# One comparison in place of two: building the one-hot rows of a scatter from a shared key table

## The reference, cut to what matters

```python
idx = jnp.take_along_axis(cand_i, best_p, axis=-1)      # first key * 128 + second key
gate = jax.nn.softmax(best_s, axis=-1)
...
act = jnp.einsum('td,thkd->thk', xb, u_tab[ib])
wgt = jax.nn.gelu(act) * gb
return jnp.einsum('thk,thkd->td', wgt, v_tab[ib])
```

## Time and profile before

| | before |
|---|---|
| median of three runs | 3481.14 us (3479.04 to 3497.25) |
| the profiled execution, its own time | 3481.03 us |
| its span in the trace | 3479.0 us |
| scatter stage of the first layer, from its first comparison to the end of its last early multiply | 1673.30 to 1767.97 us |
| scatter stage of the second layer, likewise | 2730.77 to 2825.36 us |

### The profile page before, as it was taken

How to read it: one execution, slowest core, us unless ns; L and a number is a source line. 1 busy time by engine, 2 the same in 40 slices (tenths; PEclk the granted TensorE clock), 3 DMA queues, 4 the chain that set the end, 5 groups by cost and what they waited for, 6 DMA issues and landing times. The chain is left out here.

```text
span 3479.0 us, 65019 instructions
## 1 busy us (share of the span) xinstructions
PE 3333.5 (96%) x20516; PEld 2887.0 (83%) x20516; DVE 2443.6 (70%) x4853; ACT 1766.0 (51%) x3349; POOL 522.9 (15%) x428
## 2 busy tenths in 40 slices
PE   7999999999989998999899999999999889999999
PEld 5767776778769998889778999998789778999998
DVE  6657776767566775569877777776659877777776
ACT  4443343333356655646754545444656754454544
POOL 0000000000000001558720000000648730000000
PEclk9989999999999998999999999999999999999999
DMA  5125434435215554335045555555335135555554
GB/s 206 40 76 177 164 130 133 139 121 164 73 61 175 165 175 153 110 124 173 18 139 187 187 187 187 187 187 178 122 111 169 48 109 188 187 186 187 187 187 157
DMA packets 139223, 508.82 MB, mean 146 GB/s; under 512 B 15968, under 2 KB 16352, under 8 KB 138208
## 3 DMA queue, kind: packets, MB, share of 16 engines
q1 hardware_dynamic: 138384, 504.56, 45.0%
q10 hardware_dynamic: 720, 2.71, 0.2%
HBM read 506.16 MB, written 1.05 MB: 146 GB/s over the span
## 5 line engine op out<-in xcount | busy, mean ns | idle before, releaser
L286 ACT ACTIVATE split<-ring 128x512 fp32r<-128x512 f32 (+1 forms) x1700 | 1061.4, 628 | 1393.1 <-PE ps L217 1328.5
L293 DVE TENSOR_TENSOR split<-ring,split 128x512 fp32r<-128x512 f32 (+1 forms) x1404 | 956.9, 686 | 638.5 <-ACT split L286 617.1
L217 PE MATMUL ps<-h2T,split 128*128 128x256 f32 x7776 | 982.2, 284 | 7.6 <-DVE gates L2006 4.7
L217 PEld LDWEIGHTS ps<-h2T,split 128*128 128x128 f32 x7776 | 964.9, 192 | 29.5 <-DVE gates L2006 5.1
L217 PE MATMUL ps<-split,chunk 128*128 128x512 f32 x3072 | 735.3, 391 | 2.8 <-DVE chunk L2535 2.8
L293 POOL TENSOR_TENSOR split<-ring,split 128x512 fp32r<-128x512 f32 x296 | 389.4, 1332 | 2239.9 <-ACT split L286 2233.4
L217 PEld LDWEIGHTS ps<-split,chunk 128*128 128x128 f32 x3072 | 563.8, 188 | 113.9 <-DVE chunk L2535 4.0
L217 PE MATMUL ps<-hT,split 128*128 128x512 f32 (+1 forms) x3504 | 635.9, 341 | 9.7 <-DVE split L293 5.8
L217 PEld LDWEIGHTS ps<-hT,split 128*128 128x128 f32 x3504 | 537.3, 188 | 106.2 <-DVE hT L529 13.1
L2391 PE MATMUL ps<-ring 128*128 128x128 f32 x1024 | 146.8, 288 | 42.6 <-POOL ring L2379 27.1
L217 PE MATMUL ps<-act_chunk,split 128*128 128x512 f32 (+1 forms) x1056 | 186.1, 337 | 0.0
(11 more groups left out here) (348 smaller groups left out, 3133.4 us busy)
## 6 DMA issues: line engine op xcount, KB each, us to landing
ring<-peer_uv SPq DMA_DIRECT2D x456, 512.0 KB, 3.5
ring<-w_up SPq DMA_DIRECT2D x88, 512.0 KB, 3.8
ring<-w_choose SPq DMA_DIRECT2D x88, 512.0 KB, 3.6
ring<-w_mixing SPq DMA_DIRECT2D x68, 512.0 KB, 3.5
ring<-w_merge SPq DMA_DIRECT2D x64, 512.0 KB, 4.2
ring<-w_down SPq DMA_DIRECT2D x44, 512.0 KB, 3.6
mix_row_ring<-w_mod SPq DMA_DIRECT2D x40, 512.0 KB, 3.6
ffn_row_ring<-w_mod SPq DMA_DIRECT2D x40, 512.0 KB, 4.0
```

Source lines behind the costliest of these rows:

```text
L217: ins = nc.tensor.matmul(out, lhsT(a), rhs(b), start=first and n == 0, stop=last and n == len(PASSES) - 1)
L286: self.nc.scalar.activation(self.split[:, s % SPLIT, 0, cols], self.ring[:, s, cols], ACT.Copy).then_inc(self.high_ready, 1)
L293: (ops or self.nc.vector).tensor_tensor(self.split[:, s % SPLIT, 1, cols], self.ring[:, s, cols], self.split[:, s % SPLIT, 0, cols].bitcas ...
```

## The change

First and second keys go to one table, `slot_key`, in which each lot's four first keys and four second keys lie side by side; the one-hot rows lie in one tile, `hot`, lot by lot, first four rows of first keys, then four of second keys. With this DVE compares `iota` with seven keys (896 wide) in a single instruction, which raises `one_hot` once. The eighth row stays on ACT and is now the second key of the lot's last token. POOL waits for the one comparison, as PE does.

```diff
-RAW, SPLIT = 4, 2
+RAW, SPLIT, LOT = 4, 2, 4
...
-            for n, x in enumerate((k.slot_i, k.slot_j, k.slot_gate)):
-                nc.vector.tensor_copy(x[:, :], k.ps[:, RAW + n, 0:SEQ]).then_inc(slots_ready, 1)
+            for n, x in enumerate((k.slot_key[:, :, 0, :], k.slot_key[:, :, 1, :], k.slot_gate.rearrange("p (l t) -> p l t", t=LOT))):
+                nc.vector.tensor_copy(x, k.ps[:, RAW + n, 0:SEQ].rearrange("p (l t) -> p l t", t=LOT)).then_inc(slots_ready, 1)
...
-    on_act = 1
+    many = 2 * lot - 1
...
+    slot_keys = k.slot_key.rearrange("p l s t -> p (l s t)")
...
-                for hot, slot, first in ((k.hot_i, k.slot_i, 0), (k.hot_j, k.slot_j, on_act)):
-                    many = lot - first
-                    keys = slot[:, bass.ds(token(i, n) + first, many)].unsqueeze(2).broadcast_to([P, many, NK])
-                    nc.vector.tensor_tensor(hot[:, n * lot + first:(n + 1) * lot, :], iota[:, 0:many, :], keys,
-                                            ALU.is_equal).then_inc(one_hot, 1)
+                keys = slot_keys[:, bass.ds(token(i, n) * 2, many)].unsqueeze(2).broadcast_to([P, many, NK])
+                nc.vector.tensor_tensor(k.hot[:, n, 0:many, :], iota, keys, ALU.is_equal).then_inc(one_hot, 1)
...
-                    pool.wait_ge(one_hot, (i * lots + n) * 2 + 1)
-                    hot = k.hot_i[:, n * lot:(n + 1) * lot, :]
+                    pool.wait_ge(one_hot, i * lots + n + 1)
+                    hot = k.hot[:, n, 0:lot, :]
...
-                    pe.wait_ge(one_hot, (i * lots + n) * 2 + 2)
+                    pe.wait_ge(one_hot, i * lots + n + 1)
...
-                hot = k.hot_j[:, n * lot, :]
+                hot = k.hot[:, n, 2 * lot - 1, :]
...
-                                     bias=k.slot_j[:, bass.ds(token(i, n), 1)]).then_inc(distance, 1)
+                                     bias=slot_keys[:, bass.ds(token(i, n) * 2 + 2 * lot - 1, 1)]).then_inc(distance, 1)
...
-    k.slot_i, k.slot_j, k.slot_gate = (sb(scope, f"slot_{n}", SEQ) for n in ("i", "j", "gate"))
+    k.slot_key, k.slot_gate = sb(scope, "slot_key", SEQ // LOT, 2, LOT), sb(scope, "slot_gate", SEQ)
...
-    k.hot_i, k.hot_j = hot(16, NK), hot(16, NK)
+    k.hot = Carver(k.ring.rearrange("p s m -> p (s m)"))(4, 2 * LOT, NK)
```

More of the change, by code:

```diff
@@ L2321, in _ @@
             dve.wait_ge(turned, 1)
-            for n, x in enumerate((k.slot_i, k.slot_j, k.slot_gate)):
-                nc.vector.tensor_copy(x[:, :], k.ps[:, RAW + n, 0:SEQ]).then_inc(slots_ready, 1)
+            for n, x in enumerate((k.slot_key[:, :, 0, :], k.slot_key[:, :, 1, :], k.slot_gate.rearrange("p (l t) -> p l t", t=LOT))):
+                nc.vector.tensor_copy(x, k.ps[:, RAW + n, 0:SEQ].rearrange("p (l t) -> p l t", t=LOT)).then_inc(slots_ready, 1)
 def scatter_stage(k):
-    nc, lot, lots, late = k.nc, 4, 4, NK - EARLY
+    nc, lot, lots, late = k.nc, LOT, 4, NK - EARLY
     turns_all = SEQ // (lots * lot)
-    on_act = 1
+    many = 2 * lot - 1
     iota_psum = k.ps[:, 7, 0:NK]
-    iota = iota_psum.unsqueeze(1).broadcast_to([P, lot, NK])
+    iota = iota_psum.unsqueeze(1).broadcast_to([P, many, NK])
+    slot_keys = k.slot_key.rearrange("p l s t -> p (l s t)")
     token = lambda i, n: (i * lots + n) * lot
@@ L2390, in _ @@
                     for u in range(lot):
-                        last = nc.tensor.matmul(k.ps[:, n, u * NK:(u + 1) * NK], k.hot_i[:, n * lot + u, :],
-                                                k.hot_j[:, n * lot + u, :], start=True, stop=True)
+                        last = nc.tensor.matmul(k.ps[:, n, u * NK:(u + 1) * NK], k.hot[:, n, u, :],
+                                                k.hot[:, n, lot + u, :], start=True, stop=True)
                     last.then_inc(spread, 1)
@@ L2584, in second_block @@
     k.weight = k.chunk
-    k.slot_i, k.slot_j, k.slot_gate = (sb(scope, f"slot_{n}", SEQ) for n in ("i", "j", "gate"))
+    k.slot_key, k.slot_gate = sb(scope, "slot_key", SEQ // LOT, 2, LOT), sb(scope, "slot_gate", SEQ)
     k.gelu, k.gated = sb(scope, "gelu", 2, SEQ), sb(scope, "gated", SEQ)
-    hot = Carver(k.ring.rearrange("p s m -> p (s m)"))
-    k.hot_i, k.hot_j = hot(16, NK), hot(16, NK)
+    k.hot = Carver(k.ring.rearrange("p s m -> p (s m)"))(4, 2 * LOT, NK)
     gates = sb(scope, "gates", SEQ * NK)
```

## The result

The changed kernel takes 3504.73 us (median of 15 runs, 3496.9 to 3515.96). Over the same 15 rounds the kernel before took 3485.89 us (3474.55 to 3497.25), so its earlier median of three was on the low side. The ratio is 1.0057, with a 95% interval of 1.0047 to 1.0067: the change makes the kernel slower by 0.57%, or 16 to 23 us. In the profiled executions the span went from 3479.0 to 3500.1 us.

A forecast was written before the change was run, and what follows sets the result against it. The prediction took a wait chain through DVE, POOL, PE and ACT, spanning three lots, to bound the scatter stage. Base 3481.0 plus 17.3 us (17.6 from POOL's later release, less 0.3) gave 3498.3 us, range 3490 to 3504.

The forecast's parts named there:

- the base: Starting time of the total: the profiled execution's 3481.0 us, taken as the same as the runs' median of 3481.14.
- What bounds the stage: Scatter stage: a chain DVE, POOL, PE, ACT, DVE of 4.25 us over three lots sets the pace, 1.42 us a lot.
- The comparison of 896 columns: DVE's merged comparison: 1091 ns, from a price of 1.042 ns a column given by the long rows.
- The bound from the two short rows: Upper price of DVE's merged comparison: 1.12 ns a column from the two present comparisons, 1120 ns in all.
- POOL's release and the sum: POOL waits for 896 columns, 0.40 us later; 22 links a layer give 8.8 us, 17.6 for both, less 0.3.
- a few microseconds of it at the stage's start: Part of the clock rival: low PE clock briefly at the scatter stage's start, 3500 to 3505; clock in some measure 0.08.
- The 0.5% line: Whole kernel: 17.4 us is about what a measurement can tell; forecast gap 17.2 us, 0.494%; within 0.49, slower 0.47.
- The deduction of 0.3 us: DVE's early multiplies starting right behind a comparison absorb a little of the 0.40 us: 0.3 us off the total.
- DVE as the bound with a fixed price for each instruction: Rival: DVE's work sets the scatter's pace, so fewer instructions gain: 3472 (chance 0.03), or 3462 at full fixed price (0.04).
- Hidden delay: Rival: PE's wait for POOL isn't last, so POOL's 0.4 us costs nothing, 3481 (0.03), or part, 3484 to 3495 (0.10).
- A clock drop for the whole stage: Rival: PE's longer gaps bring 1.2 GHz throughout the scatter, up to 3546; clock in some measure, 3502 to 3546, 0.08.
- Contention: Rival: DVE's new comparison slowed by POOL's work to 3 us, total over 3550; given no chance.

The follow-up runs named there:

- a3: Changed kernel with its comparison cut into five rows, then two, POOL waiting for the first alone: ratio 1.0026, stages of 97.0 and 98.3 us.
- a2: Changed kernel with two comparisons, three second keys first, then four first keys, POOL waiting for both: ratio 1.006, stages of 105.8 and 105.4 us.
- c3: a2 with DVE's early columns three lots late and ACT's copy two lots late: ratio 0.9939, stages of 83.5 and 83.6 us.
- c1: Kernel before with DVE's early columns three lots late and ACT's copy two lots late: ratio 0.991, stages of 83.6 and 83.5 us.
- c2: Changed kernel with DVE's early columns three lots late and ACT's copy two lots late: ratio 0.9921, stages of 82.9 and 82.7 us.
- a1_split43: Changed kernel with its comparison cut into four first keys, then three second keys, POOL waiting for the first alone: ratio 0.9988, stages of 95.9 and 93.9 us.
- d2_held_clock: c2 with three idle multiplications ahead of PE's first matmul of the stage: ratio 0.9917, stages of 80.8 us in both layers.

## Why the prediction's mechanism was right, and which term was wrong

The forecast was 3498.3 us with a range of 3490 to 3504, and the measured 3504.73 lies above it. The step that failed is the first term of the total, the base of 3481.0 us: it is 4.9 of the 6.4 us by which the forecast is off. The mechanism held, and the cost of the change, 17.3 us, came out at 18.1 in the two stages.

**What bounds the stage: right.** That a chain through four engines and no engine's work sets the pace was shown by moving it. It lengthens with each column ahead of POOL (a3, a2, the change), and with one number of DVE's order and one of ACT's it goes away, and with it what POOL's late release costs in the steady part (c3).

**The comparison of 896 columns: right.** 1091 ns expected from the long rows, 1091 seen. The bound from the two short rows (1120) was too high.

**POOL's release and the sum: right in kind, a little small.** The first step grew by 0.40 us in the mean, as expected, and three lots together by 0.40 to 0.41 (from the paces of lots 8 to 60). The sum gave 17.3 us and the stages show 18.1; the medians differ by 18.8 and the ratio says 16 to 23. What the sum lacks against the stages is a term that I had at nothing in the likeliest case, the clock at the stage's start. In the second layer PE's first 24 records took 4.59 us, as before the change (4.54), and the stage came out at 103.2 us, where 94.6 + 17.3 / 2 = 103.3 was expected. In the first they took 5.5 (4.4 before), and the stage 104.2, some 0.8 us above the 103.3. How long the low clock lasts differs from layer to layer within one kernel (below), so one profile doesn't show that this term belongs to the change. The case "a few microseconds of it at the stage's start" stood among the rivals at 3500 to 3505. That the measured time lies just in that range is luck: in the profile the clock was worth under 1 us, and most of the way there is the error of the base.

**The base: wrong.** "3481.0 + 17.3" took the profiled execution as the middle of the runs, and the median of three, 3481.14, as "the same for this purpose". The kernel before takes 3485.89 us in the median of 15 runs, 4.9 more, and 3485.89 + 17.3 = 3503.2, inside my range. The range to 3504 was made of errors of the sum alone and had no room for one of the base, though the three runs before spanned 18 us. Most of this spread probably lies in the other stages: over the kernels here, each profiled once, the rest of the span varied by 25 us, while the scatter's stage differed between two layers of one kernel by at most 2 us where DVE's early columns are two lots late.

**The 0.5% line.** I put the forecast a hair below it and gave 0.49 to "within" and 0.47 to "slower". The interval (0.47 to 0.67%) lies nearly all above. The deduction of 0.3 us for the early multiplies that start right behind a comparison was too small to matter (the second layer came out as the sum has it, to 0.1 us), while the effects left out, the clock above all, could only add.

**Rivals.** DVE as the bound with a fixed price for each instruction: no, the two-instruction form with a late POOL (a2) is as slow as the change. But where DVE sets the pace (c1 against c2), one instruction less is worth 0.7 us a layer. Whether DVE is full is what decides. Hidden delay: no, the columns ahead of POOL showed in full. A clock drop for the whole stage: no, it was 1.00 at 72% busy. Contention: no, the median of the 128 comparisons is 1092 ns.

## What to carry to other kernels

When no engine is full, follow one item round through all engines until it releases the next, count how many items that loop spans, and divide: here 4.25 us over three lots. In such a loop merging instructions helps only behind the point where another engine is released; put what the next engine waits for first, or split it off. The cheap cure is to let the loop span one item more (a number in the order of work, with the buffers already there), and only when the engine that runs them is full is it worth saving an instruction. Take the base of a forecast from as many runs as there are, and put their spread into the range.

## What was not expected of the hardware

The low clock behind PE's idle time before the stage isn't the same from layer to layer of one kernel. In a1_split43, behind 2.98 and 2.97 us of idleness, PE's first records of the stage took (in time order, PE's first stretch in each layer)

```profile
1675.91 7.86 PE L2391 MATMUL ps<-ring 128*128 128x128 f32 x40 [2.98 <-POOL ring L2379]
...
2734.58 2.19 PE L2391 MATMUL ps<-ring 128*128 128x128 f32 x16 [2.97 <-POOL ring L2379]
```

The rows count different numbers of records. Like for like, PE's first 24 records took 5.46 us in the first layer and 3.53 in the second, and its first 16 took 3.75 and 2.19. The last is close to the 2.13 us that d2_held_clock needs for 16 at a clock of 1.00. It is 2 us of a stage.

In c1, where DVE has no idle time in the steady part, the comparison of 512 columns took 731 ns in the median (692 before) and the early multiply 308 (270), with the starts no further apart (0.60 us from the first comparison to the second, 0.61 before). In c2, with DVE nearly as full, neither duration rose (1087 and 264 ns). What causes it was not tried.
